# Feed-forward up in a two-layer encoder trunk: tokens instead of weights as the stationary operand, rows turned by VectorE and small DMAs

## The chip, the cores and the metric

The kernel runs on one core of one Trainium2 chip. The metric is the device time of one execution in microseconds (us); the time of the kernel before is the median of three runs. The profile is one more execution, recorded by the hardware profiler. Engines are named as in the profile: PE is TensorE, and PEld its loading of stationary operands; DVE is VectorE, ACT ScalarE, POOL GpSimd, and SP (SPq in the trace) is SyncE, which here issues nearly all DMAs.

## What is computed

Two layers, each with a mixer beside a cross-attention into 256 memory tokens, an output projection and a feed-forward part. Only the feed-forward part is touched: 256 tokens, width 2048, hidden width 8192, all float32.

```python
for layer in range(2):
    ...                                   # mixer, memory attention, output projection
    hn = rmsnorm(h, ffn_norm_g[layer])
    h = h + jnp.square(jax.nn.relu(hn @ ffn_w1[layer])) @ ffn_w2[layer]
return rmsnorm(h, final_norm_g)
```

## The kernel before

**Precision.** Each float32 operand is split into a high and a low float32r part, and each product is made of three matmuls: high by high, high by low, low by high. For weights, ACT writes the high part `w_hi` from the landed tile `raw` (`split`, L1072, the instruction is at L1077), and DVE subtracts to get `w_lo` (`split`, L1602, L1607).

**The weight stream.** SP loads weights as 128x512 tiles of 256 KB (`load`, L388; the DMA is at L397) into eight slots. Sixteen tiles (k-tiles, kt 0 to 15, eight slabs s of two) make a block. The load of k-tile kt waits until PE has used the k-tile eight before it (`tile_used`, L396). So SP runs at most eight k-tiles ahead of PE, and ACT and DVE follow, each strictly in program order: `head(B)` splits slabs 0 and 1 of block B, `tail(B)` slabs 2 to 7.

**The feed-forward part of a layer** (`ffn`; L957 on PE, L1486 on ACT, L2202 on DVE, L2397 on POOL; `stream_ffn`, L408, on SP) has two halves of 4096 hidden units. Each half has eight *up* blocks (512 hidden units each, 16 k-tiles) and eight *down* blocks (four column groups of two blocks). `R_FFN` and `B_FFN` number results and blocks.

- *Up* (`up_slab`, L552): the weight tile is the stationary operand, in four 128x128 pieces f. For each k-tile and piece there is a matmul of 512 columns (`w_hi` against high and low tokens side by side, L565) and one of 256 columns (`w_lo` against high tokens, L567). The result has hidden units on partitions and tokens along the row, as down wants it. Even blocks (j = 0) take all four result banks, odd blocks (j = 1) the four `aux` banks (`up_bank`, L325).
- *After an up block*: ACT copies the high-token half out of each of the four banks (`up_highs`, L1471, L1476), DVE adds the other half (`relu_result`, L2143, L2148) and applies relu and the tokens' 1/rms (L2158). That factor is needed along the row, so it is spread once per layer by two matmuls against a diagonal (`rstd_rows`, L571). POOL squares a 128x1024 tile (L2395), ACT writes its high part `hid_hi` (`hidden`, L1482) and DVE the low part `hid_lo` (`hidden`, L2172), during the next block.
- *Down* (`slab`, L534): the hidden tokens are stationary (128x128), and the weight tile streams as 512 columns; per k-tile six matmuls of 512 columns (two token halves m by three products, L546 to L548). Results go to two of four banks by turns, and DVE adds them into `h` (`add_result`, L2165).

The first up block of a layer (`first_up`) stands beside the last transposes of the normalised tokens (`refill`). `slab` is also what all other projections of the kernel use, with the tokens `xT_hi`, `xT_lo` as stationary operand.

Of the kernel before, what the change touches and what calls it, by code (L numbers as in the profile page):

```python
# [14 lines left out]
P = 128  # L15
D = 2048
SEQ = 256
# [96 lines left out]
A_RS0 = A_FN0 + 8  # L114
A_TN1 = A_RS0 + 1
# [5 lines left out]
A_RS = (A_RS0, A_FN1 + 8)  # L121
# [35 lines left out]
def encoder_trunk(nc, x, mem, x_columns, mem_columns, mem_gain_columns, consts, tok_norm_g, dn_w_in, dn_conv_w, dn_a_log, dn_dt_bias,  # L157
# [13 lines left out]
    with ctx:  # L171
# [127 lines left out]
        up_T = relu[:].rearrange("p j m (f t) -> p j (m f) t", f=2)  # L299
# [25 lines left out]
        def up_bank(R, j, f):  # L325

            return aux[f] if j else banks[(2 * (R % 2) + f) % 4]
# [59 lines left out]
        def _(sp):  # L387
# [20 lines left out]
            def stream_ffn(layer):  # L408
                with sp.Fori(0, 2) as half:
                    with sp.Fori(0, 8) as i:  # L410
                        for s in range(SLABS):
                            load(ffn_w1[layer], 0, half * (HID // 2) + i * NB, half * 16 + i + B_FFN[layer], s)
                    with sp.Fori(0, 4) as i:
                        for s in range(2 * SLABS):
                            B = half * 16 + i * 2 + (B_FFN[layer] + 8 + s // 8)
                            load(ffn_w2[layer], half * (HID // 2) + (s // 8) * D, i * NB, B, s % 8)

# [115 lines left out]
        def _(pe):  # L533
# [17 lines left out]

            def up_slab(B, s, R, parity, j, odd=None):  # L552

                for k in range(2):
                    kt = 2 * s + k
                    slot = kt % SLOTS
                    pe.wait_ge(tiles_split, B * 16 + (kt + 1))
                    for f in range(4):
                        if kt == 0 and j == 0:
                            pe.wait_ge(result_drained[f % 2], R + (f // 2 + 1))  # L560
                        elif kt == 0 and f == 0:
                            pe.wait_ge(sem("up_aux_free"), odd)
                        acc = up_bank(parity, j, f)
                        cols = slice(f * P, (f + 1) * P)
                        pe.matmul(acc[:], w_hi[:, slot, cols], xT[:, kt], start=kt == 0, stop=False,  # L565
                                  skip_group_check=True)
                        mm = pe.matmul(acc[:, 0:SEQ], w_lo[:, slot, cols], xT_hi[:, kt, :], start=False, stop=kt == KT - 1,  # L567
                                       skip_group_check=True)
                    mm.then_inc(tile_used, 1)

            def rstd_rows(layer):  # L571

                n = A_RS[layer]
                may_fill(pe, n)
                pe.wait_ge(sem("rstd_diagonal"), 2 * layer + 2)
                for m in range(2):
                    mm = pe.matmul(aux[n % 4][:, m * P:(m + 1) * P], ones, rstd_diag[:, m], start=True, stop=True)
                mm.then_inc(aux_filled[n % 4], 1)

            def first_up(layer):  # L580

                for s in range(SLABS):
                    drained(pe, ffn_fill[layer][s])
                    if s == SLABS - 1:
                        rstd_rows(layer)
                    up_slab(B_FFN[layer], s, R_FFN[layer], R_FFN[layer], 0)
                    yield
# [358 lines left out]
            def last_gates():  # L946

                for s in range(SLABS):
# [6 lines left out]
                         first_up(0)))  # L955

            def ffn(layer, next_steps, next_fill=None):  # L957


                for half in range(2):  # L960
                    def up(it, j):
                        b = it * 2 + j
                        for s in range(SLABS):
                            up_slab(half * 16 + b + B_FFN[layer], s, half * 12 + b + R_FFN[layer], R_FFN[layer], j,
                                    half * 16 + it * 4 + (32 * layer + 4) if j else None)
                    if half == 1:
                        up(0, 0)
                    if half == 0:
                        for n in range(4):
                            drained(pe, A_RS[layer] - n)  # L970
# [26 lines left out]
                    def down(i, c):  # L997

                        for s in range(16):
                            if (i, c) == (0, 0) and s % 2 == 0:  # L1000
                                pe.wait_ge(sem("hidden_split"), 16 * layer + 8 * half + s // 2 + 3)
# [61 lines left out]
            for n in (1, 2):  # L1063
                finish(out_block(n))
            beside(refill(ffn_fill[1], h, REFILL, R_OUT[1]),
                   chain(out_block(3), first_up(1)))
# [4 lines left out]
        def _(act):  # L1071
# [385 lines left out]
            def first_up(layer):  # L1457

                for t in range(SLABS):
                    split(B_FFN[layer] + (t + 2) // 8, (t + 2) % 8)  # L1460
                    if t == SLABS - 3:
                        norm_known(act, (N_FFN0, N_FFN1)[layer])
                        for m in range(2):
                            act.activation(rstd_diag[:, m], ident, ACT.Copy, scale=rstd[:, 0, m:m + 1]
                                           ).then_inc(sem("rstd_diagonal"), 1)
                    if t == SLABS - 1:
                        copy_aux(A_RS[layer], rstd_row, src=aux[A_RS[layer] % 4][:, 0:SEQ])
                        up_highs(layer, B_FFN[layer], 16 * layer, 0)
                    yield

            def up_highs(layer, B, n, j):  # L1471

                act.wait_ge(sem("hidden_split"), n + 1)
                result(act, B)
                for f in range(4):
                    act.activation(up_T[:, j, f, :], up_bank(R_FFN[layer], j, f)[:, 0:SEQ], ACT.Copy  # L1476
                                   ).then_inc(sem("up_high"), 1)

            beside(refill(ffn_fill[0], GN_FFN, REFILL_OUT, R_FFN[0]),
                   chain(out_part(8 * B_OUT[0] + 24, 8), first_up(0)))  # L1480

            def hidden(layer, half, it, j):  # L1482
                act.wait_ge(sem("squared"), half * 8 + it * 2 + (16 * layer + j + 1))
                act.activation(hid_hi[:, bass.ds(it * 8 + 4 * j, 4), :], up_T[:, j], ACT.Copy).then_inc(sem("hidden_hi"), 1)

            def ffn(layer, stages=None, next_steps=None):  # L1486
                for half in range(2):
                    def up(it, j, between):
                        tail(half * 16 + it * 2 + (B_FFN[layer] + j), between)
                        head(half * 16 + it * 2 + (B_FFN[layer] + j + 1))  # L1490
                        up_highs(layer, half * 16 + it * 2 + (B_FFN[layer] + j), half * 8 + it * 2 + (16 * layer + j), j)
                    if half == 1:
                        up(0, 0, None)
                    with act.Fori(0, 3) as it:
                        up(it, 1, lambda: hidden(layer, half, it, 0))
                        up(it + 1, 0, lambda: hidden(layer, half, it, 1))
                    up(3, 1, lambda: hidden(layer, half, 3, 0))
                    B = half * 16 + B_FFN[layer] + 8
                    tail(B, lambda: hidden(layer, half, 3, 1))
                    if half == 0:  # L1500
                        with act.Fori(0, 7) as i:
                            head(i + (B + 1))
                            tail(i + (B + 1))
                        head(B + 8)
                for i in range(3):
                    head(B + 1)
                    tail(B + 1)
                    head(B + 2)
# [67 lines left out]
            for n in (1, 2):  # L1576
                finish(block_steps(B_OUT[1] + n))
            beside(refill(ffn_fill[1], GN_FFN + 16, REFILL, R_FFN[1]),
                   chain(block_steps(B_OUT[1] + 3), first_up(1)))
# [14 lines left out]
        def _(dve):  # L1594
# [4 lines left out]
            dve.sem_inc(sem("up_aux_free"), 4)  # L1599
            dve.sem_inc(sem("hidden_split"), 2)  # L1600
# [542 lines left out]
            def relu_result(layer, n, R, j):  # L2143

                drained(dve, A_RS[layer])
                for f in range(4):
                    dve.wait_ge(sem("up_high"), 4 * n + (f + 1))
                    e = dve.tensor_tensor(up_T[:, j, f, :], up_T[:, j, f, :], up_bank(R_FFN[layer], j, f)[:, SEQ:], ALU.add)  # L2148
                    if j == 0:
                        free_result(e, f % 2)  # L2150
                    else:
                        e.then_inc(sem("up_aux_free"), 1)
                if j == 0:
                    for m in range(2):
                        dve.wait_ge(result_drained[m], R + 4)
                else:
                    dve.wait_ge(sem("up_aux_free"), 2 * n + 6)
                dve.scalar_tensor_tensor(out=up_T[:, j], in0=up_T[:, j], scalar=0.0, in1=over(rstd_row, 4),  # L2158
                                         op0=ALU.max, op1=ALU.mult).then_inc(sem("activated"), 1)

# [280 lines left out]
```

## Time and profile before

| | |
|---|---|
| median of 3 runs | 2309.48 us (2309.35 to 2315.8) |
| span of the profiled execution | 2308.9 us |
| PE busy | 2295.0 us, 99% |
| DVE, ACT, POOL busy | 1531.6 (66%), 1231.1 (53%), 114.3 us (5%) |
| HBM read | 419 MB, 182 GB/s over the span |
| granted TensorE clock | 0.999 of full speed (2.4 GHz) |

The span runs from the first to the last instruction of the profiled execution; its time and the median of the runs differ by 0.6 us. The page is read from the busy shares to the chain that ended last, then to the groups of instructions by line, and then, stage by stage, to the order of time.

### The profile page before, as it was taken

The numbers are of one execution on the slowest core, as the hardware profiler recorded it, in microseconds if no ns is written. First come the engines' busy times: TensorE is split into PE (matmuls) and PEld (weight loads), VectorE is DVE, ScalarE is ACT, GpSimd is POOL, SyncE is SP. The second block draws the span as 40 slices with busy tenths as digits, with TensorE's granted clock in tenths as the row PEclk, the third lists the DMA queues.
The fourth block names the chain that finished last, engine by engine and source line by source line (L and its number), as shares of the span: only waits on it lengthen the run. The fifth ranks groups of instructions, "written<-read, shape, count | busy, mean of one in ns | idle before, by whom it ended". The sixth has DMA issues, their size and how long they took to land.

```text
span 2308.9 us, 35429 instructions
## 1 busy us (share of the span) xinstructions
PE 2295.0 (99%) x11661; PEld 1945.0 (84%) x11661; DVE 1531.6 (66%) x2513; ACT 1231.1 (53%) x2277; POOL 114.3 (5%) x90
## 2 busy tenths in 40 slices
PE   9999999999999999999999999999999999999998
PEld 7888888888888888888888888888888888888887
DVE  6678788797767755567665555556767555677555
ACT  6566475564555544455544455545555444555544
POOL 0010100000001100001000000000101000001000
PEclk9999999999999999999999999999999999999999
DMA  9655364463566666666666675666666666666665
GB/s 327 185 156 163 112 170 140 134 185 111 162 189 188 190 193 193 192 186 185 185 193 194 188 214 158 168 190 196 188 189 190 193 194 192 189 190 189 194 193 176
DMA packets 232549, 422.82 MB, mean 183 GB/s; under 512 B 27884, under 2 KB 29805, under 8 KB 232301
## 3 DMA queue, kind: packets, MB, share of 16 engines
q1 hardware_dynamic: 231709, 420.15, 61.1%
q8 instruction: 77, 1.26, 0.2%
q10 hardware_dynamic: 720, 1.06, 0.1%
q14 instruction: 43, 0.35, 0.0%
HBM read 419.00 MB, written 2.10 MB: 182 GB/s over the span
## 4 chain that ended last, share of the span: by engine, by line
PE 94%; DVE 3%; ACT 1%; DMA 1%; issue 0%; SPq 0%; POOL 0%; POOLq 0%; ACTq 0%; DVEq 0%
PE pair L546 19%; PE pair L548 19%; PE pair L547 19%; PE pair L565 10%; PE aux L565 10%; PE aux L567 5%; PE pair L567 5%; PE aux L776 3%; PE aux L594 2%; DVE w_lo L1607 1%; DMA raw<-in_mem_w_kv 1%; DVE r L1934 1%; PE aux L823 0%; DVE attnT L1928 0%; DVE projections L1834 0%
## 5 line engine op out<-in xcount | busy, mean ns | idle before, releaser
L1607 DVE TENSOR_TENSOR w_lo<-raw,w_hi 128x512 fp32r<-128x512 f32 x1536 | 1077.6, 728 | 583.6 <-ACT w_hi L1077 580.9
L1077 ACT ACTIVATE w_hi<-raw 128x512 fp32r<-128x512 f32 x1536 | 939.9, 634 | 778.9 <-DMA raw<-in_ffn_w 619.9
L546 PE MATMUL pair<-w_hi,hid_hi 128*128 128x512 f32 x1012 | 394.3, 390 | 0.0
L548 PE MATMUL pair<-w_hi,hid_lo 128*128 128x512 f32 x1012 | 393.8, 389 | 0.0
L547 PE MATMUL pair<-w_lo,hid_hi 128*128 128x512 f32 x1012 | 393.8, 389 | 0.0
L546 PE MATMUL pair<-w_hi,xT 128*128 128x512 f32 x960 | 384.0, 400 | 3.3 <-DVE w_lo L1607 2.4
L548 PE MATMUL pair<-w_hi,xT 128*128 128x512 f32 x960 | 374.6, 390 | 0.0
L547 PE MATMUL pair<-w_lo,xT 128*128 128x512 f32 x960 | 374.1, 390 | 0.0
L565 PE MATMUL pair<-xT,w_hi 128*128 128x512 f32 x1024 | 359.6, 395 | 0.4 <-DVE h L2170 0.2
L565 PE MATMUL aux<-xT,w_hi 128*128 128x512 f32 x1024 | 357.4, 394 | 0.0
L567 PE MATMUL pair<-xT,w_lo 128*128 128x256 f32 x1024 | 286.3, 280 | 0.0
L567 PE MATMUL aux<-xT,w_lo 128*128 128x256 f32 x1024 | 286.2, 279 | 0.0
L565 PEld LDWEIGHTS pair<-xT,w_hi 128*128 128x128 f32 x1024 | 191.9, 187 | 46.4 <-DVE h L2170 2.2
L565 PEld LDWEIGHTS aux<-xT,w_hi 128*128 128x128 f32 x1024 | 191.8, 187 | 44.2
L548 PEld LDWEIGHTS pair<-w_hi,hid_lo 128*128 128x128 f32 x1012 | 189.9, 188 | 39.9
L546 PEld LDWEIGHTS pair<-w_hi,hid_hi 128*128 128x128 f32 x1012 | 190.0, 188 | 39.2
L547 PEld LDWEIGHTS pair<-w_lo,hid_hi 128*128 128x128 f32 x1012 | 190.0, 188 | 39.1
L546 PEld LDWEIGHTS pair<-w_hi,xT 128*128 128x128 f32 x960 | 180.5, 188 | 43.4 <-issue 5.1
L548 PEld LDWEIGHTS pair<-w_hi,xT 128*128 128x128 f32 x960 | 180.2, 188 | 38.7
L547 PEld LDWEIGHTS pair<-w_lo,xT 128*128 128x128 f32 x960 | 180.7, 188 | 34.4
L567 PEld LDWEIGHTS pair<-xT,w_lo 128*128 128x128 f32 x1024 | 193.2, 189 | 0.1
L567 PEld LDWEIGHTS aux<-xT,w_lo 128*128 128x128 f32 x1024 | 193.2, 189 | 0.0
(265 smaller groups left out, 1463.3 us busy)
## 6 DMA issues: line engine op xcount, KB each, us to landing
raw<-in_ffn_w SPq DMA_DIRECT2D x1024, 256.0 KB, 3.0
raw<-in_dn_w_in SPq DMA_DIRECT2D x208, 256.0 KB, 2.9
raw<-in_tok_w_out SPq DMA_DIRECT2D x128, 256.0 KB, 3.0
raw<-in_gm_w_in SPq DMA_DIRECT2D x112, 256.0 KB, 2.9
raw<-in_mem_w_kv SPq DMA_DIRECT2D x64, 256.0 KB, 3.2
r<-in_mem_columns SPq DMA_DIRECT2D x8, 256.0 KB, 5.6
h<-in_x_columns SPq DMA_DIRECT2D x8, 256.0 KB, 7.2
h<-in_mem_columns SPq DMA_DIRECT2D x8, 256.0 KB, 3.3
```

The lines of the kernel that those rows point to most:

```text
L546: pe.matmul(acc, act_hi[:, kt, tokens], w_hi[:, slot], start=start, stop=False)
L547: pe.matmul(acc, act_hi[:, kt, tokens], w_lo[:, slot], start=False, stop=False)
L548: mm = pe.matmul(acc, act_lo[:, kt, tokens], w_hi[:, slot], start=False, stop=last and k == 1)
L565: pe.matmul(acc[:], w_hi[:, slot, cols], xT[:, kt], start=kt == 0, stop=False, skip_group_check=True)
L567: mm = pe.matmul(acc[:, 0:SEQ], w_lo[:, slot, cols], xT_hi[:, kt, :], start=False, stop=kt == KT - 1, skip_group_check=True)
L594: t = pe.transpose(aux[n % 4][0:src.shape[1], col:col + w], src, cst[0:w, C_ID:C_ID + w])
L776: mm = pe.matmul(bank(n)[part, i * width:(i + 1) * width], lhs(i), rhs(i), start=True, stop=True)
L1077: act.activation(w_hi[:, slot], raw[:, slot], ACT.Copy).then_inc(hi_ready, 1)
L1607: dve.tensor_tensor(w_lo[:, slot], raw[:, slot], w_hi[:, slot].bitcast(F32), ALU.subtract).then_inc(tiles_split, 1)
L1934: e = dve.scalar_tensor_tensor(out=NT[:, d, m, hh, :], in0=view[:, k, 1, :], scalar=beta(m, d, hh), in1=NT[:, d, m, hh, :], op0=ALU.mult, ...
```

## The change

Up uses `slab`, the same six matmuls of 512 columns per k-tile as down, with the tokens stationary and the weights streaming. So an up result has tokens on partitions and hidden units along the row, in two banks by turns. What follows has to turn it:

- ACT evicts a result with relu and 1/rms in two 128x512 instructions (at s = 2 of the next block), into `up_rows`.
- POOL squares them in place, in two 128x512 halves.
- DVE transposes 32x32 squares of each half into `turned_rows` (at s = 5 and 6 of that next block).
- SP moves 32x32 squares between partition groups: 16 DMAs per block (`move_hidden`), each of 32 partitions with 1 KB, from `turned_rows` to `hidden_T`. They stand in SP's queue behind slabs 1 to 4 of the block two later, four at a time, and the first waits for both transposes. The last two blocks of a half are moved during the first two down blocks.
- ACT then writes `hid_hi` in two 128x512 halves (at s = 3 of the block two later, behind a wait for all 16 DMAs), and DVE `hid_lo` in two halves (at s = 4).

`rstd_rows`, `up_slab`, `first_up`, `up_highs` and `relu_result` are gone, and the `aux` slot of the spread factor too.

```diff
-        up_T = relu[:].rearrange("p j m (f t) -> p j (m f) t", f=2)
+        up_rows = relu[:].rearrange("p j m n -> p j (m n)").rearrange("p j (f m c) -> p j f m c", f=4, m=2)
+        turned_rows = xn_late[:, 0].rearrange("p (j a f m i) -> p j f m a i", j=2, a=4, f=4, m=2)
+        hidden_T = xn_late[:, 1].rearrange("p (j b f m i) -> p j m f b i", j=2, b=4, f=4, m=2)
...
@@ sync, stream_ffn @@
+                    with sp.Fori(0, 3) as it:
+                        for j in range(2):
+                            for s in up(it * 2 + (2 + j)):
+                                if 1 <= s < 5:
+                                    move_hidden(block_of(layer, half, j) + it * 2, half, j, s - 1)
+                    for s in down(0):
+                        if 1 <= s % 8 < 5:
+                            move_hidden(block_of(layer, half, 6 + s // 8), half, s // 8, s % 8 - 1)
...
+            def move_hidden(n, half, j, part):
+                if part == 0:
+                    sp.wait_ge(sem("rows_turned"), 2 * n + 2)
+                a = part
+                turned, moved = (xn_late[:, m, j * 2 * NB:(j + 1) * 2 * NB].rearrange("p (c y) -> p c y", c=4) for m in range(2))
+                for b in range(4):
+                    dst, src = moved[32 * a:32 * a + 32, b], turned[32 * b:32 * b + 32, a]
+                    sp.dma_start(dst, src).then_inc(sem(f"hidden_moved{half}{j}"), 16)
...
@@ tensor, ffn @@
-                            up_slab(half * 16 + b + B_FFN[layer], s, half * 12 + b + R_FFN[layer], R_FFN[layer], j,
-                                    half * 16 + it * 4 + (32 * layer + 4) if j else None)
+                            slab(b + (half * 16 + B_FFN[layer]), s, b + (half * 12 + R_FFN[layer]),
+                                 (R_FFN[layer] + j) % 2, 2 * s, xT_hi, xT_lo, s == 0, s == SLABS - 1)
...
@@ scalar @@
+            def up_tail(layer, half, B, last=None, before=None):
+                for s in range(2, SLABS):
+                    split(B, s)
+                    if s == 2 and last is not None:
+                        it, j = last
                         norm_known(act, (N_FFN0, N_FFN1)[layer])
+                        result(act, it * 2 + (half * 16 + B_FFN[layer] + j))
                         for m in range(2):
...
+                            rows = banks[2 * ((R_FFN[layer] + j) % 2) + m][:].rearrange("p (f c) -> p f c", f=4)
+                            free_result(act.activation(up_rows[:, j, :, m, :], rows, ACT.Relu, scale=rstd[:, 0, m:m + 1]), m)
+                    if s == 3 and before is not None:
+                        it, j = before
+                        act.wait_ge(sem(f"hidden_moved{half}{j}"), it * 256 + (1024 * layer + 256))
+                        tiles = hid_hi[:, bass.ds(it * 8 + 4 * j, 4), :].rearrange("p f (m b i) -> p m f b i", m=2, b=4)
+                        for m in range(2):
+                            act.activation(tiles[:, m], hidden_T[:, j, m], ACT.Copy).then_inc(sem("hidden_hi"), 1)
...
@@ vector @@
+            def up_tail(layer, half, B, last=None, before=None):
+                for s in range(2, SLABS):
+                    split(B, s)
+                    if s == 4 and before is not None:
+                        it, j = before
+                        high, low = (x[:, bass.ds(it * 8 + 4 * j, 4), :].rearrange("p f (m b i) -> p m f b i", m=2, b=4)
+                                     for x in (hid_hi, hid_lo))
+                        for m in range(2):
+                            dve.wait_ge(sem("hidden_hi"), it * 4 + (2 * block_of(layer, half, j) + m + 1))
+                            dve.tensor_tensor(low[:, m], hidden_T[:, j, m], high[:, m].bitcast(F32), ALU.subtract
+                                              ).then_inc(sem("hidden_split"), 1)
+                    if s in (5, 6) and last is not None:
+                        it, j = last
+                        m = s - 5
+                        dve.wait_ge(sem("squared"), it * 4 + (2 * block_of(layer, half, j) + m + 1))
+                        dve.transpose(turned_rows[:, j, :, m], up_rows[:, j, :, m, :].rearrange("p f (a i) -> p f a i", a=4)).then_inc(sem("rows_turned"), 1)
...
@@ gpsimd, square_hidden @@
+                            for m in range(2):
+                                pool.wait_ge(result_drained[m], half * 12 + it * 2 + (R_FFN[layer] + j + 3))
+                                t = up_rows[:, j, :, m, :]
+                                pool.tensor_tensor(t, t, t, ALU.mult).then_inc(sem("squared"), 1)
```

## Rows read from the trace of the kernel before

**Rows 1.** The page: engines' busy time, and the chain that ended last, by engine

```profile
PE 2295.0 (99%) x11661; PEld 1945.0 (84%) x11661; DVE 1531.6 (66%) x2513; ACT 1231.1 (53%) x2277; POOL 114.3 (5%) x90
...
PE 94%; DVE 3%; ACT 1%; DMA 1%; issue 0%; SPq 0%; POOL 0%; POOLq 0%; ACTq 0%; DVEq 0%
```

**Rows 2.** Order of time, PE, inside an up block: start, length (us), instruction

```profile
700.22 0.40 PE L565 MATMUL aux<-xT,w_hi 128*128 128x512 f32 x1
700.45 0.28 PE L567 MATMUL aux<-xT,w_lo 128*128 128x256 f32 x1
700.57 0.39 PE L565 MATMUL aux<-xT,w_hi 128*128 128x512 f32 x1
```

**Rows 3.** Single lines' instructions, and PE's order of time: starts of the stages

```profile
L565 PE MATMUL pair<-xT,w_hi x256: 392/395/500, 619.8 to 777.2; 128*128 128x512 f32 x128
...
L546 PE MATMUL pair<-w_hi,hid_hi x512: 389/389/481, 799.7 to 1331.7; 128*128 128x512 f32 x171
...
973.82 0.39 PE L565 MATMUL pair<-xT,w_hi 128*128 128x512 f32 x1
...
1155.30 0.40 PE L546 MATMUL pair<-w_hi,hid_hi 128*128 128x512 f32 x1
...
L565 PE MATMUL pair<-xT,w_hi x13: 389/398/496, 1594.8 to 1599.7; 128*128 128x512 f32 x13
...
L546 PE MATMUL pair<-w_hi,hid_hi x9: 387/389/391, 1774.4 to 1779.9; 128*128 128x512 f32 x9
...
L565 PE MATMUL pair<-xT,w_hi x64: 389/391/497, 1948.5 to 1971.0; 128*128 128x512 f32 x64
...
L546 PE MATMUL pair<-w_hi,hid_hi x244: 387/389/391, 2126.6 to 2291.9; 128*128 128x512 f32 x122
```

**Rows 4.** Order of time, PE, around the spread of 1/rms

```profile
641.18 0.60 PE L577 MATMUL aux<-rstd_both,cst 128*128 128x128 f32 x4
641.54 0.48 PE L565 MATMUL pair<-xT,w_hi 128*128 128x512 f32 x1
```

**Rows 5.** Who waited for whom: engine, line, releaser, total us, times, longest

```profile
PEld pair L565 <- DVE h L2170: 2.2, 6, 0.5
```

**Rows 6.** Line L397 in seven up blocks: SP's issues (ns min/median/max) and landing

```profile
L397 SPq DMA_DIRECT2D raw<-in_ffn_w x112: 332/333/343, 644.7 to 798.7; - x112
...
DMA to landing us min/median/max: 2.7/2.9/3.9
```

**Rows 7.** Order of time, SP, in the first 45 us: issues behind one another

```profile
2.59 0.91 SPq L397 DMA_DIRECT2D raw<-in_mem_w_kv  x2
...
7.18 0.74 SPq L435 DMA_DIRECT2D tok<-in_tok_norm_g  x1
7.96 0.42 SPq L435 DMA_DIRECT2D tok<-in_ffn_norm_g  x1
...
8.80 0.30 SPq L435 DMA_DIRECT2D tok<-in_gm_b_s  x1
9.14 0.37 SPq L436 DMA_DIRECT2D tok<-in_dn_conv_w  x1
...
43.32 0.43 SPq L459 DMA_DIRECT2D rows<-in_dn_a_log  x1
43.79 0.43 SPq L459 DMA_DIRECT2D rows<-in_dn_dt_bias  x1
```

**Rows 8.** Groups by line and shape: busy us, mean ns, idle before

```profile
L1607 DVE TENSOR_TENSOR w_lo<-raw,w_hi 128x512 fp32r<-128x512 f32 x1536 | 1077.6, 728 | 583.6 <-ACT w_hi L1077 580.9
L1077 ACT ACTIVATE w_hi<-raw 128x512 fp32r<-128x512 f32 x1536 | 939.9, 634 | 778.9 <-DMA raw<-in_ffn_w 619.9 <-DMA raw<-in_tok_w_out 55.6 <-DMA raw<-in_dn_w_in 42.1
...
L2395 POOL TENSOR_TENSOR relu<-relu 128x1024 f32<-128x1024 f32 x32 | 72.8, 2275 | 976.7 <-DVE relu L2158 976.7
...
L2158 DVE SCALAR_TENSOR_TENSOR relu<-relu,rstd_both 128x1024 f32<-128x1024 f32 x32 | 39.2, 1225 | 2.8 <-DVE relu L2148 0.9
```

**Rows 9.** Stretches: busy us by engine, granted clock, DMA share, GB/s (an up stage)

```profile
619.80:799.70 179.90, 179.90 (x1043) 157.31 (x1042) 127.86 (x182) 98.01 (x176) 17.42 (x9) 1.00 0.65 187
```

More of the change, by code:

```diff
@@ L113 @@
 A_FN0 = A_MIX0B + 2
-A_RS0 = A_FN0 + 8
-A_TN1 = A_RS0 + 1
+A_TN1 = A_FN0 + 8
 A_WS = A_TN1 + 8
@@ L323, in encoder_trunk, with block_of @@
         tok1_fill = [A_TN1 + p for p in range(8)]
-        def up_bank(R, j, f):
-            return aux[f] if j else banks[(2 * (R % 2) + f) % 4]
+        def block_of(layer, half, b):
+            return 16 * layer + 8 * half + b
         def filled(e, n, rounds=0):
@@ L550, in slab @@
                     mm.then_inc(tile_used, 1)
[L552 to L587, printed above, removed]
             def transposes(n, pieces, rounds=0):
@@ L1455, in _ @@
                                                 out_part(8 * B_OUT[0], 24)))
[L1457 to L1461, printed above, removed]
+            beside(refill(ffn_fill[0], GN_FFN, REFILL_OUT, R_FFN[0]),
+                   chain(out_part(8 * B_OUT[0] + 24, 8), block_steps(B_FFN[0])))
+            def up_tail(layer, half, B, last=None, before=None):
[3 more added lines that the diff above has]
+                        it, j = last
@@ L1469, in first_up @@
[L1469 to L1480, printed above, removed]
@@ L1486, in ffn, with up @@
             def ffn(layer, stages=None, next_steps=None):
                 for half in range(2):
[L1488 to L1491, printed above, removed]
+                    def up(b, last, before=None):
+                        up_tail(layer, half, b + (half * 16 + B_FFN[layer]), last, before)
+                        head(b + (half * 16 + B_FFN[layer] + 1))
@@ L1498, in ffn @@
                     B = half * 16 + B_FFN[layer] + 8
-                    tail(B, lambda: hidden(layer, half, 3, 1))
+                    up_tail(layer, half, B, (3, 1), (3, 0))
+                    head(B + 1)
+                    up_tail(layer, half, B + 1, None, (3, 1))
+                    head(B + 2)
                     if half == 0:
[L1501 to L1504, printed above, removed]
+                        with act.Fori(0, 6) as i:
+                            tail(i + (B + 2))
+                            head(i + (B + 3))
@@ L2141, in _ @@
             residual(dve, R_OUT[0] + 4)
[L2143 to L2159, printed above, removed]
             beside(refill(ffn_fill[0], GN_FFN, REFILL_OUT, 48, R_FFN[0]),
                    chain(out_part(PART_B, 8 * B_OUT[0] + 24, R_OUT[0] + 4),
-                         block_steps(B_FFN[0], lambda: relu_result(0, 0, R_FFN[0], 0))))
+                         block_steps(B_FFN[0])))
             def add_result(B, parity, i):
```

100 lines of the change are left out of this document (43 added, 57 removed).

## The prediction

> **What bounds the kernel now.** I read the page first: PE is busy for 99% of the span and carries 94% of the chain that ended last; no other engine is over 66% [rows 1]. So time can only be won by giving PE less to do, and is lost wherever PE has to wait. Next the order of time inside an up block [rows 2]: a 512-column matmul starts 0.23 us before its 256-column neighbour, and that one 0.12 us before the next. The lengths in that view overlap (0.40 and 0.28); only the distance of the starts is what a matmul costs. Last, the starts of the eight feed-forward stages [rows 3], which give the same distances as means over hundreds of matmuls.
>
> Layer 1, second up stage: 1948.5 to 2126.6, 178.1 us for 8 blocks x 16 k-tiles x 4 pieces = 512 pairs, 0.3479 us a pair. Layer 1, first down stage: 1774.4 to 1948.5, 174.1 us for 8 x 16 x 6 = 768 matmuls of 512 columns, 0.2267 us each. Both multiply the same number of columns (4 x 768 = 6 x 512 = 3072 per k-tile). At 2.4 GHz, the level granted there [rows 9], 512 columns are 213.3 ns and 768 are 320 ns. What stands over is 13.4 ns for one matmul and 27.9 ns for two: nearly the same for each instruction, whatever its width. Up pays it eight times per k-tile, down six times.
>
> **Part by part: PE.** Up becomes the six matmuls of down. Per k-tile 4 x 0.3479 = 1.392 us become 6 x 0.2267 = 1.360 us. By stages: 178.1 becomes 174.1, a gain of 4.0, in three of four up stages. In the second half of layer 0 both stages ran at a slower pace (973.8 to 1155.3 is 181.5; 1155.3 to 1332.4, three matmuls after its last high one, is 177.1): a gain of 4.4 there. Together 16.4 us. The matmuls that spread 1/rms go, 0.36 us in each layer [rows 4]: 0.7. An even up block needs all four result banks, so at the start of a second half it waits for DVE's `add_result`: 2.2 us in six waits of the weight loads [rows 5], mostly beside running matmuls. They go too, as `slab` needs only the two banks that are free; but since they are inside the 178.1 that I also applied to first halves, which have none, I take 0.5 off. **Sum on PE: 16.6 us**, if PE never waits. The span would go from 2308.9 to 2292.3, the median, which lies 0.6 higher, from 2309.5 to 2292.9.
>
> Here a rule speaks against the change. The Trainium skill (TensorE: Matmul & The Clock Gate, section "Back-to-back issue gap") gives the spacing of lone matmuls as N/2.4 + 2.5 ns, so 2.5 ns an instruction instead of some 14; worked out from that page, two matmuls fewer in each of 512 k-tiles would be worth an estimated 2.6 us. The trace disagrees: 226.7 ns measured where the formula gives 215.8.
>
> **Part by part: what feeds PE.** Everything else lies beside PE as long as the weight tiles keep coming. POOL: two squares of about 2.275 / 2 = 1.14 us [rows 8] instead of one; they start when ACT has evicted, some 2 us into the next block, and DVE wants them near 14 us: covered. If squares were late, DVE and then SP would be. ACT: two evictions and two halves of `hid_hi` at about 0.63 each, where four copies and one 128x1024 stood; no more work. DVE loses four additions and two passes of 1.23 per block, and gains two halves of `hid_lo` at 0.73 and two transposes. No row shows a transpose: the bounds are 0.73 (a 128x512 on DVE) and 1.23 (a 128x1024, if it runs at half pace) [rows 8]; a gain against 0.73 is excluded as it passes as many elements. I take 0.73, the row of equal shape.
>
> SP's queue is the new place. Before, it held 16 weight issues a block, 0.33 us each, in 21.8 us [rows 6]. Now 16 moves stand between them, four behind each of slabs 1 to 4, behind a wait for DVE's transposes. Queued behind that wait and the moves are the weight loads of k-tiles 4 to 15, for which ACT, DVE and PE wait. An issue behind another took 0.47 us (43.32 to 43.79), at the least 0.34 (8.80 to 9.14), at the most 0.78 (7.18 to 7.96); two weight loads took 0.91 and a gap of 0.04, so 0.475 each [rows 7]. I take 0.47 for a move, from issues with nothing slow ahead of them. 16 x 0.47 + 16 x 0.475 = 15.1 us of 21.8: it fits in sum. What matters is a **closed loop**, passed once a block: transposes done, moves, landing, `hid_hi`, `hid_lo`, next transposes. Each engine works in program order, so weight splits lie in it as well:
>
> - SP: 15 issues of 0.47 ahead of the last move, and six weight loads (k-tiles 4 to 9): 7.05 + 2.85 = 9.9.
> - Landing of the last move: 2.9, the median for weights (2.7 to 3.9) [rows 6]. No row shows a move inside SBUF; for less and for more I keep these ends.
> - ACT: two halves of `hid_hi` 1.27, splits of k-tiles 8 and 9 1.27.
> - DVE: split of k-tile 9 0.73, `hid_lo` 1.46, k-tiles 10 and 11 1.46, transpose 0.73, k-tiles 12 and 13 1.46, transpose 0.73.
>
> Sum 21.9 us, against a block of 16 x 1.360 = 21.8. So the loop is as long as the block itself. How long PE stays fed: k-tile 9 is loaded when k-tile 1 has been used, 2.7 us into the block, so the last move is issued near 4.7 and lands at 7.6; `hid_hi` ends at 8.9; DVE has split k-tile 9 at 11.0, `hid_lo` is done at 12.4 and k-tile 10 split at 13.15. PE wants it at 10 x 1.36 = 13.6: a slack of about 0.5 us. With e the loop's excess over 21.8, and seven passes from the first to the last of a half's eight blocks, a half loses 7e - 0.5. For e = 0.14 that is 0.5 us, 1.9 us over four halves. **Forecast: 2292.9 + 1.9 = 2295 us.**
>
> Its own bounds: a loop with moves of 0.34 is 2 us shorter and leaves 2293; a loop of 22.1 (e = 0.35) gives 7 x 0.35 - 0.5 = 2 per half, 2301. Without the slow pace of layer 0's second half (3.4 + 3.0 us in the two stages) the lower end is 2288.
>
> **The rivals.**
> *The loop sets the pace (slower).* It decides where a half loses its gain of 4.15: 7e - 0.5 = 4.15, e = 0.66, a loop of 22.4 us. Either upper end does this alone: transposes of 1.23 or a landing of 3.9 add 1.0, so e = 1.14, 7.5 us a half, 30 in all: 2323. Moves of 0.63, halfway to the upper end, add 2.4: e = 2.54, 17.3 a half, 2362; moves of 0.78 would give 2425. For it: the sum itself has no slack, and SP never had to issue so many. Against: 0.74 stands only where a slow DMA was ahead, and the quick rows (0.30, 0.37) are small transfers like the moves.
> *Part of the gain is eaten.* The same loop with e from 0.35 to 0.66: 2301 to 2309.
> *The DMA engines are the bound.* A block's moves add 16 x 32 = 512 pieces of 1 KB to 16 x 128 = 2048 of 2 KB. With a price per piece the DMA share goes from 0.65 [rows 9] to 0.81, with a price per byte to 0.73: neither is 1, so I expect only later landings. At 3.9 for weights, k-tile 8 (issued at 2) is there at 6 and waits for ACT until 8.9 anyway. If it bound nevertheless it would show as the loop's landing at 3.9: 2323. The Trainium skill (DMA: Bandwidth & Descriptors, section "Measured (HBM→SBUF, 128 partitions, SWDGE, issued from GpSimd)") says that transfers under 64 KB are ruled by their descriptors and wants 1 MiB; the moves are 32 KB. No run here shows such a transfer.
> *The change doesn't do what it says.* If a matmul's overhead went with its columns, 0.3479 would already be 1.5 x 0.2267 = 0.340 plus waiting that the new form keeps; then only the spread and the start waits are won: 2309.5 - 0.7 - 2 = 2307. Against it: two stretches of hundreds of matmuls agree on 13 to 14 ns each. The formula of the Trainium skill above would end in the same place.
>
> **How the numbers follow.** Forecast (2288 to 2301) 0.60; part eaten (2301 to 2309) 0.13; loop sets the pace, with the DMA engines as its cause among it, 0.24, most of it at 2312 to 2362; change without effect (2307) 0.03. About 0.3% (7 us) is what a measurement of this kernel can tell from no change. Faster than 2302.6: 0.60 and a little of the second case, 0.63. Within: the rest of the second, the fourth, and 0.04 of the third, 0.17. Slower than 2316.4: 0.20. The range goes from 2288 to 2316 and leaves out 0.20 above.
>
> **What would show it.** Right: up stages of 174 to 176 us, a first-to-first distance of 0.227 in them, ACT's wait for the moves at s = 3 ending before PE runs dry, PE's idle time still near nothing. Wrong on the price of a matmul: the distance is over 0.23 in up with no waits. Wrong on the loop: PE waits for `w_lo` of k-tiles 8 to 12 in blocks 2 to 7 of a half and in its first two down blocks; SP's move issues over 0.55, their landing over 3.5, or transposes over 1 us tell which term it was. What would make the prediction wrong most likely is SP's issue time for moves.

## The result, and the profile after

The changed kernel takes 2364.5 us (2361.7 to 2364.9), the kernel before 2310.8 in the same runs: a ratio of 1.0224, 95% interval 1.0209 to 1.0239. It is 2.2% slower. The forecast was 2295, and 2364 lies above the range's upper end of 2316; it is where the first rival put moves of 0.63 us (2362).

The page of the changed kernel: busy time, the chain that ended last (by engine, by line), three groups of instructions, and the moves' DMA issues (median us to landing).

```profile
span 2363.0 us, 32922 instructions
PE 2293.0 (97%) x10629; PEld 1899.5 (80%) x10629; DVE 1432.3 (61%) x2449; ACT 1233.8 (52%) x2239; POOL 106.9 (5%) x122
...
PE 73%; SPq 13%; DVE 4%; DMA 3%; ACT 3%; issue 3%; POOL 0%; ACTq 0%; POOLq 0%; DVEq 0%
PE pair L572 23%; PE pair L574 22%; PE pair L573 22%; SPq L442 9%; SPq L397 3%; PE aux L765 3%; DMA xn_late<-xn_late 3%; PE aux L583 2%; DVE w_lo L1584 2%; ACT hid_hi L1462 1%; ACT w_hi L1063 1%; DVE r L1911 1%; DMA raw<-in_mem_w_kv 1%; PE aux L812 0%; DVE attnT L1905 0%
...
L572 PE MATMUL pair<-w_hi,xT 128*128 128x512 f32 x1984 | 788.8, 398 | 46.8 <-DVE w_lo L1584 45.9
...
L1462 ACT ACTIVATE hid_hi<-xn_late 128x512 f32 (+1 forms) x64 | 36.8, 622 | 133.3 <-DMA xn_late<-xn_late 133.3
L2147 DVE STREAM_TRANSPOSE xn_late<-relu 128x512 f32<-128x512 f32 x64 | 45.0, 703 | 0.0
...
xn_late<-xn_late SPq DMA_DIRECT2D x512, 32.0 KB, 2.3
```

Against [rows 1], PE's share of the chain fell from 94% to 73%, and SP's queue, which had none, now holds 13%: 9% of it in line L442, the moves. The span outside PE's busy time was 13.9 us before and is 70.0 now. The next lines say who waits (total us, times, longest): PE for DVE's low weight parts, in 37 waits where the kernel before (first line) had 5, and ACT for the moves, once for each of the 32 up blocks. Of the 37, 32 lie in the feed-forward part, eight in each half.

```profile
PE pair L546 <- DVE w_lo L1607: 3.3, 5, 1.4
...
PE pair L572 <- DVE w_lo L1584: 59.8, 37, 3.3
...
ACT hid_hi L1462 <- DMA xn_late<-xn_late: 133.3, 32, 5.8
```

One block of the chain, in order of time (start, length, what), from where PE gets k-tile 8 after a wait to where it gets k-tile 8 of the next block. Matmuls, moves and loads between are left out.

```profile
701.75 0.70 DVE w_lo L1584
702.50 0.50 PE pair L572
...
708.03 0.24 PE pair L574
708.42 0.33 SPq L397
708.90 0.53 SPq L442
709.47 0.59 SPq L442
710.11 0.59 SPq L442
710.74 0.59 SPq L442
711.60 0.35 SPq L397
712.20 0.34 SPq L397
712.59 0.51 SPq L442
...
721.10 0.59 SPq L442
721.73 1.83 DMA xn_late<-xn_late
723.86 0.38 issue
724.24 0.61 ACT hid_hi L1462
724.85 0.53 ACT w_hi L1063
725.40 0.70 DVE w_lo L1584
726.14 0.50 PE pair L572
```

The pass takes 726.14 - 702.50 = 23.64 us, where PE alone needs 21.76 for a block. PE uses k-tiles 8 to 11 (24 matmuls, 5.8 us); that lets SP load k-tile 3 of the next block (708.42); then SP issues 15 moves and six loads in a row (708.90 to 721.73); the sixteenth move lands 1.83 us after its issue began; ACT, which stands at the moves, makes `hid_hi`, then splits k-tile 8; DVE splits it; PE goes on. Behind another move, a move's issue starts 0.62 to 0.64 us later (709.47, 710.11, 710.74), against 0.47 in [rows 7]; 0.625 is what the sums below take.

DVE's second transposes, those of the moves in this pass and those of the next pass, were done at 707.87 and 731.51:

```profile
707.17 0.70 DVE L2147 STREAM_TRANSPOSE xn_late<-relu 128x512 f32<-128x512 f32 x1
...
730.81 0.70 DVE L2147 STREAM_TRANSPOSE xn_late<-relu 128x512 f32<-128x512 f32 x1
```

### The profile page after: what moved, and what is told of

Its sections match the earlier page's. It is cut to its first block, busy times and chain, and to the rows that moved or that the text cites. A ratio compares the mean times of both kernels' runs of the same rounds, so it can differ in the third digit from the quotient of the medians.

```text
span 2363.0 us, 32922 instructions
## 1 busy us (share of the span) xinstructions
PE 2293.0 (97%) x10629; PEld 1899.5 (80%) x10629; DVE 1432.3 (61%) x2449; ACT 1233.8 (52%) x2239; POOL 106.9 (5%) x122
## 4 chain that ended last, share of the span: by engine, by line
PE 73%; SPq 13%; DVE 4%; DMA 3%; ACT 3%; issue 3%; POOL 0%; ACTq 0%; POOLq 0%; DVEq 0%
PE pair L572 23%; PE pair L574 22%; PE pair L573 22%; SPq L442 9%; SPq L397 3%; PE aux L765 3%; DMA xn_late<-xn_late 3%; PE aux L583 2%; DVE w_lo L1584 2%; ACT hid_hi L1462 1%; ACT w_hi L1063 1%; DVE r L1911 1%; DMA raw<-in_mem_w_kv 1%; PE aux L812 0%; DVE attnT L1905 0%
## 5 line engine op out<-in xcount | busy, mean ns | idle before, releaser
L1584 DVE TENSOR_TENSOR w_lo<-raw,w_hi 128x512 fp32r<-128x512 f32 x1536 | 1025.3, 693 | 803.5 <-ACT w_hi L1063 798.8
L572 PE MATMUL pair<-w_hi,xT 128*128 128x512 f32 x1984 | 788.8, 398 | 46.8 <-DVE w_lo L1584 45.9
L574 PE MATMUL pair<-w_hi,xT 128*128 128x512 f32 x1984 | 776.1, 391 | 0.0
L573 PE MATMUL pair<-w_lo,xT 128*128 128x512 f32 x1984 | 775.7, 391 | 0.0
L572 PEld LDWEIGHTS pair<-w_hi,xT 128*128 128x128 f32 x1984 | 374.5, 189 | 136.5 <-DVE w_lo L1584 57.2
L574 PEld LDWEIGHTS pair<-w_hi,xT 128*128 128x128 f32 x1984 | 374.1, 189 | 79.9
L573 PEld LDWEIGHTS pair<-w_lo,xT 128*128 128x128 f32 x1984 | 374.9, 189 | 74.3
L2373 POOL TENSOR_TENSOR relu<-relu 128x512 f32<-128x512 f32 x64 | 65.3, 1042 | 1033.0 <-ACT relu L1456 1033.0
L2147 DVE STREAM_TRANSPOSE xn_late<-relu 128x512 f32<-128x512 f32 x64 | 45.0, 703 | 0.0
L1811 DVE SCALAR_TENSOR_TENSOR r<-r,conv_w 128x256 f32<-128x256 f32 x96 | 40.0, 480 | 6.7 <-ACT r L1251 6.7
L2141 DVE TENSOR_TENSOR hid_lo<-xn_late,hid_hi 128x512 f32 (+1 forms) x64 | 41.1, 684 | 0.0
L1456 ACT ACTIVATE relu<-pair,rstd 128x512 f32<-128x512 f32 x64 | 40.0, 676 | 0.0
L1105 ACT ACTIVATE xT<-aux,gains 128x256 fp32r<-128x256 f32 x48 | 19.8, 472 | 33.7 <-PE aux L583 33.7
```

Of the source, the lines that this page charges most:

```text
L572: pe.matmul(acc, act_hi[:, kt, tokens], w_hi[:, slot], start=start, stop=False)
L573: pe.matmul(acc, act_hi[:, kt, tokens], w_lo[:, slot], start=False, stop=False)
L574: mm = pe.matmul(acc, act_lo[:, kt, tokens], w_hi[:, slot], start=False, stop=last and k == 1)
L1584: dve.tensor_tensor(w_lo[:, slot], raw[:, slot], w_hi[:, slot].bitcast(F32), ALU.subtract).then_inc(tiles_split, 1)
L2147: dve.transpose(turned_rows[:, j, :, m], up_rows[:, j, :, m, :].rearrange("p f (a i) -> p f a i", a=4)).then_inc(sem("rows_turned"), 1)
L2373: pool.tensor_tensor(t, t, t, ALU.mult).then_inc(sem("squared"), 1)
```

## The experiments

Two theories stood first. **A**: the time is SP's, 16 issues in a row at 0.6 us, with weight loads queued among them and ACT's splits queued behind the wait for them. **B**: it is the DMA engines', the moved bytes. All times below are beside runs of the kernel before on the same chip.

**Leaving the moves out** (`e1_no_moves`). The first down blocks and DVE's `hid_lo` are changed in the same way.

```diff
-                                    move_hidden(block_of(layer, half, j) + it * 2, half, j, s - 1)
+                                    pass
...
-                        act.wait_ge(sem(f"hidden_moved{half}{j}"), it * 256 + (1024 * layer + 256))
+                        act.wait_ge(sem("rows_turned"), it * 4 + (2 * block_of(layer, half, j) + 2))
...
-                            act.activation(tiles[:, m], hidden_T[:, j, m], ACT.Copy).then_inc(sem("hidden_hi"), 1)
+                            act.activation(tiles[:, m], turned_rows[:, j, :, m], ACT.Copy).then_inc(sem("hidden_hi"), 1)
```

> The 16 moves per block are left out (the high and low hidden parts are made from the turned rows, so squares stand in wrong partition groups); all else stays. Theory A, SP's queue: in the changed kernel 16 issues of about 0.6 us and the landing of the last hold ACT ahead of k-tile 8, and nothing else is lost; without them up runs at down's pace: 2292 to 2297. Theory B, the moves' bytes load the DMA engines: the same here. Theory C, the price of a matmul was wrong, or transposes and squares in program order hold DVE up: 2305 or more, with PE waits left in up blocks.

Measured: 2289.4 us against 2312.7, ratio 0.9901 (0.9884 to 0.9918), 2.6 us below the expected band. Busy time, and a down stage and the up stage behind it, each from its first matmul to the next stage's (length, then busy us of PE, PEld, DVE, ACT and POOL, granted clock, DMA share, GB/s):

```profile
PE 2273.2 (99%) x10629; PEld 1895.3 (83%) x10629; DVE 1473.5 (64%) x2449; ACT 1238.0 (54%) x2239; POOL 106.9 (5%) x122
...
793.75:967.83 174.08, 174.08 (x770) 144.19 (x769) 95.82 (x140) 83.76 (x134) 2.04 (x2) 1.00 0.63 194
967.83:1141.90 174.07, 174.07 (x769) 144.19 (x768) 109.77 (x156) 93.86 (x154) 14.29 (x14) 1.00 0.68 193
```

Up and down take the same 174.1 us, PE is busy throughout. So the evictions, squares, transposes and half-width copies cost PE no time, the gain on PE is there in full, and all 75 us between 2289 and 2364 hang on the moves. In the two profiles the span differs by 76.3 us (2363.0 against 2286.7): 56.5 is more time without a matmul (70.0 against 13.5), 19.8 is longer matmuls (2293.0 against 2273.2 busy), of which more below.

**How many, and how large** (`e3_eight_moves`, `e10_twelve_moves`, `e4_half_bytes`, `e14_twenty_moves`). Fewer moves leave out the last two, or the last, of each four (`for b in range(2)`, `range(3)`); the half-size run moves 128 elements a row instead of 256; the last one adds a fifth:

```diff
                     sp.dma_start(dst, src).then_inc(sem(f"hidden_moved{half}{j}"), 16)
+                sp.dma_start(spare[32 * a:32 * a + 32, :], turned[0:32, a, 0:HALF]).then_inc(sem(f"hidden_moved{half}{j}"), 16)
```

> Eight of the 16 moves per block are left out (half of the hidden values are stale), each of the rest as large as before. Theory A: eight issues of 0.62 us fewer, 5.0 us, more than the 1.9 us by which a block is too long: no PE waits are left, 2293 to 2297. Theory B: half the moved bytes are left, so about half of the 70 us: near 2330.

> Four of the 16 moves per block are left out (a quarter of the hidden values are stale). By theory A, with a point from which it decides: the loop shrinks by 4 x 0.625 = 2.5 us, more than its excess of 1.9, so the whole loss goes and not a quarter: 2289 to 2296. If each move cost the same 70 / 16 = 4.4 us: 2347.

> All 16 moves per block stay, but each carries 512 bytes per partition instead of 1 KB (half of the hidden values are stale). Theory A: the number of issues sets the time, so 2358 to 2366. Theory B, bytes: near 2330, as with eight moves.

> The changed kernel with four more moves per block, one behind each of slabs 1 to 4 (64 elements a row, into a spare tile that nobody reads). Theory A: past the point from which the loop decides, each issue costs its whole time: 4 x 0.625 = 2.5 us a block, some 28 to 32 passes, so 70 to 80 us more: 2430 to 2445. If SP's queue still had room, or if the bytes counted (6% more): within 10 us of 2364.

| moves per block | bytes per block | us (before in the same runs) |
|---|---|---|
| 0 | 0 | 2289.4 (2312.7) |
| 8 | 256 KB | 2289.3 (2312.7) |
| 12 | 384 KB | 2291.8 (2309.7) |
| 16, as changed | 512 KB | 2364.5 (2310.8) |
| 16, half rows | 256 KB | 2359.2 (2312.7) |
| 20 | 544 KB | 2484.9 (2313.1) |

Eight moves and sixteen half moves carry the same bytes, and differ by 70 us: B falls. (Eight came out 4 us below the expected band, twelve and the half moves inside theirs.) Twelve moves are nearly free and sixteen cost 75 us: there is a point from which the loop decides, and it lies between. Past it, four more moves cost 120 us where A had 70 to 80. The profile of that run shows why. The span outside PE's busy time grew by 74.8 us (144.8 against 70.0), as A had it; the other 46.4 are PE's busy time (2339.4 against 2293.0): after the longer waits its matmuls themselves ran slower (last section). A block there takes 27.7 us, 4.0 more and not 2.5 (PE's 24 matmuls of k-tiles 8 to 11 take 7.4 us of it, 735.87 to 743.23, instead of 5.8), as SP's order of time shows (the first moves of two blocks), and the last line is the stretch of one block (length, then busy us of PE, PEld, DVE, ACT and POOL, granted clock, DMA share, GB/s):

```profile
716.18 2.45 SPq L443 DMA_DIRECT2D xn_late<-xn_late  x4
...
743.87 2.41 SPq L443 DMA_DIRECT2D xn_late<-xn_late  x4
...
724.00:748.00 24.00, 19.99 (x81) 16.13 (x80) 11.71 (x19) 10.28 (x18) 2.04 (x2) 0.93 0.57 171
```

**Using the moved rows later** (`e2_late_wait`). Every move stays where it was; ACT comes to them at s = 6 and DVE at s = 7, behind the transposes (s = 5 and 6 in the last block of a half).

```diff
-                    if s == 3 and before is not None:
+                    if s == (5 if early else 6) and before is not None:
...
-                    if s == 4 and before is not None:
...
+                    if s == (6 if early else 7) and before is not None:
```

> All moves stay, where they were in SP's queue; only their use is put later in the block: the high hidden part at s = 6 (5 in the second down block) instead of 3, the low part at s = 7 (6) instead of 4, behind the transposes. Theory A1, the loss is ACT's wait for the moves, which stands ahead of the weight splits of k-tiles 8 and 9: that wait falls to nearly nothing, PE wants k-tile 10 at 13.6 us and has it at about 13.0: 2293 to 2302. Theory A2, the loss is SP's issues alone, which bring the weight tiles late whoever waits: at least half of the 70 us between 2293 and 2364 stays, 2330 or more. Theory B, DMA engines: the landing of weights and moves stays what it was, 2330 or more.

Measured: 2307.8 us against 2312.7, ratio 0.9977 (0.9968 to 0.9987), above the expected band. Of the 75 us, 57 go, with no DMA taken away: what cost most was the place of the use, ACT's weight splits behind a wait for the moves. (DVE's order was changed with it; the run `e13_early_turn` below changes DVE's order alone, and gains nothing.) The rest is seen in who PE waited for:

```profile
PE pair L572 <- DVE w_lo L1584: 7.7, 17, 1.4
PE pair L572 <- DVE hid_lo L2146: 7.3, 4, 2.1
```

The four waits for `hid_lo` are the last block of each half, used too late by my own edit. The 17 for `w_lo` are the other part (four of them, 3.0 us, stand in the run without moves too): SP takes 3.69 us for four moves and two loads (708.90 to 712.59 in the chain above), PE uses the two k-tiles in 2.72, so loads fall behind whoever waits.

**Spreading them** (`e11_spread`). The late use, with three moves behind each of slabs 1 to 5 and one behind slab 6, and the last block of a half used at s = 4 and 5.

```diff
+                for k in range(each * (s - 1), min(each * s, 16)):
+                    a, b = k // 4, k % 4
```

> All moves and the late use, with two edits: three moves behind each of slabs 1 to 5 and one behind slab 6, instead of four behind each of 1 to 4 (a group then takes SP 3.1 us per slab instead of 3.7; PE uses a slab in 2.7), and the last block of a half used at s = 4 and 5 instead of 5 and 6. Theory A: the weight tiles fall behind by 5 x 0.4 = 2 us instead of 4 x 0.95 = 3.8, and the 17 waits for low weight parts of the late-use run (17 us) and the four for the last hidden part (9 us) go: 2289 to 2297. If the rest of the loss in that run had another cause than SP's pace: 2303 or more.

Measured: 2289.4 us against 2309.7, ratio 0.9914 (0.9895 to 0.9933): the whole loss is gone with nothing left out.

**Other queues** (`e7_two_queues`, `e5_pool_queue`). In the first, SP keeps moves b = 0 and 1, and ACT issues b = 2 and 3, four behind each of its splits of slabs 0 and 1; their use stays where the change put it. In the second, GpSimd issues all 16, behind its squares.

```diff
+                for s, parts in ((0, (0, 1)), (1, (2, 3))):
+                    split(B, s)
+                    if last is not None:
+                        move_rest(j, half, parts)
```

> The same 16 moves of the same bytes, and their use where the change put it; but eight of them are issued from ACT's queue, behind its splits of slabs 0 and 1. ACT has 9 us a block free and pays 8 x 0.6 = 5 of them. Theory A, issues in a row on SP: SP's part of the loop shrinks by 5.0 us as with eight moves, 2289 to 2297, with nothing left out. Theory B, the engines behind the queues: no better than 2355. Rival: ACT, in program order, gets too late with its splits: PE waits for the low weight parts of k-tiles 2 to 6, 2310 or more.

> All 16 moves go from SP's queue to GpSimd's, which has 20 us a block free; their use stays where the change put it. Theory A: SP is as free as before; if an issue there takes up to 0.6 us, the last lands as late as now but no weight tile does, and only ACT's wait is left: 2300 to 2350. If GpSimd's issues take 1 us or more, 16 of them are the loop: 2400 or more. Theory B, engines: 2364 as now.

Measured: 2288.8 us against 2309.7, ratio 0.9910 (0.9891 to 0.9929) with two queues (at the lower end of the band); 2295.0, ratio 0.9937 (0.9913 to 0.9962), with GpSimd's. GpSimd's issues were quicker than I had allowed for, as its order of time shows (start, length, engine, line):

```profile
699.22 7.87 POOL L2369 DMA_DIRECT2D xn_late<-xn_late  x16 [9.26 <-DVE xn_late L2137]
```

That is 0.49 us each, so the last one lands early, and the time is below the expected band. Same moves, same bytes; what differs is whose time the issues take, and that the moves no longer stand between weight loads. Landing was no quicker: medians of 2.7 and 3.0 us from SP and ACT, and 2.9 from GpSimd, against 2.3 in the changed kernel. This settles A against B. The Trainium skill (DMA: Bandwidth & Descriptors, section "Issuing engines are not separate DMA queues") says that issuing from several engines only saves the sequencers' time, usually small beside the DMA; the first half agrees with both runs, and the second does not hold here, where an issue took 0.59 us of the 2.3 until a move landed, and the issues together 16 x 0.625 = 10 us of a 21.8 us block.

The GpSimd run is 6 us behind the other (5.6 between the profiles), and this lies behind the work: PE's last matmul ends at 2279.5 us in it and at 2279.1 in the two-queue run, but the program's last instructions come behind GpSimd's closing DRAIN, which takes 11.1 us (2281.2 to 2292.4) where it takes 0.67 in the two-queue run:

```profile
L169 POOLq DRAIN  x1: 11131/11131/11131, 2281.2 to 2281.2; - x1
...
L169 POOLq DRAIN  x1: 665/665/665, 2280.9 to 2280.9; - x1
```

**Which loop** (`e13_early_turn`). Only the transposes are moved forward.

```diff
-                    if s in (5, 6) and last is not None:
+                    if s in (3, 4) and last is not None:
                         it, j = last
-                        m = s - 5
+                        m = s - 3
```

> The changed kernel with only DVE's two transposes moved forward, to s = 3 and 4 instead of 5 and 6; nothing is left out. The loop of the prediction ran through the transposes (transposes, moves, landing, high part, low part, four splits, transposes): if it is the one that sets the pace, it gets 4 splits, 2.7 us, shorter, and the time falls to 2300 or less. Theory A as the trace of the changed kernel reads: SP stands at k-tile 3 until PE has used the k-tile eight earlier, and the transposes are done by then: no change, 2358 to 2368.

Measured: 2370.5 us against 2313.1, ratio 1.0249 (1.0219 to 1.0279), 2 us above the expected band. A block takes 23.9 us, from the first move of one block in SP's queue to that of the next:

```profile
708.65 2.43 SPq L442 DMA_DIRECT2D xn_late<-xn_late  x4
...
732.59 2.41 SPq L442 DMA_DIRECT2D xn_late<-xn_late  x4
```

There is no gain (the interval overlaps that of the changed kernel, so a loss is not shown either): the transposes, and with them the loop of the prediction, do not set the pace.

**What a move's issue costs, and why** (`e12_prices`). The two-queue kernel, and behind its last store five groups of four DMAs, issued by SP with nothing else running.

```diff
+            price("price_groups", [(raw[32:64, i, 0:256], xn_late[64:96, 0, i * 256:(i + 1) * 256]) for i in four])
+            price("price_same", [(raw[32:64, i, 256:512], xn_late[32:64, 0, i * 256:(i + 1) * 256]) for i in four])
+            price("price_all", [(raw[:, i, 0:256], xn_late[:, 0, i * 256:(i + 1) * 256]) for i in four])
+            price("price_hbm32", [(raw[0:32, 4 + i, 0:256], ffn_w1[0][32 * i:32 * i + 32, 0:256]) for i in four])
+            price("price_hbm128", [(raw[:, 4 + i], ffn_w1[0][P * i:P * i + P, 0:NB]) for i in four])
```

> The two-queue kernel, and behind its last store five groups of four DMAs, each group issued in a row by SP and waited for, with nothing else running: 32 rows of 1 KB from SBUF to SBUF between partition groups (a move), the same inside one group, 128 rows of 1 KB from SBUF to SBUF, 32 rows of 1 KB from HBM, 128 rows of 2 KB from HBM. It adds some 20 us at the end, which is not what is asked. Why did a move's issue take 0.59 us and not the 0.43 of the rows before? If it is the place (both ends in SBUF), the first three groups take 0.5 to 0.6 each and the last two 0.33 to 0.43. If it is the small number of rows, groups 1, 2 and 4 are at 0.5 to 0.6. If it is the other partition group, only the first. If it is the busy queue in the middle of the kernel, all are below 0.45.

The run's time holds the five groups and is not compared. Issues in stretches of its end (ns min/median/max, first and last start), one line for each group in that order:

```profile
L558 SPq DMA_DIRECT2D raw<-xn_late x1: 592/592/592, 2288.7 to 2288.7; - x1
...
L558 SPq DMA_DIRECT2D raw<-xn_late x3: 507/590/592, 2291.2 to 2292.4; - x3
...
L558 SPq DMA_DIRECT2D raw<-xn_late x3: 601/601/602, 2295.5 to 2296.8; - x3
...
L558 SPq DMA_DIRECT2D raw<-in_ffn_w x3: 421/421/423, 2299.3 to 2300.3; - x3
...
L558 SPq DMA_DIRECT2D raw<-in_ffn_w x2: 432/432/432, 2302.9 to 2303.3; - x2
```

Behind another one, an issue from SBUF to SBUF takes 0.59 to 0.60 us, with 32 rows or 128, inside a partition group or between two; from HBM 0.42 to 0.43, with 32 rows or 128. It is the place, not the rows, the partition group, or the busy kernel around it. And it is both places together, not the source alone: the kernel's own stores go from SBUF to HBM, and SP's four of them took 0.33 to 0.42 us in this run:

```profile
L554 SPq DMA_DIRECT2D out<-xn_late x4: 332/382/423, 2278.8 to 2283.3; - x4
```

## Why the prediction was wrong, step by step

- **The price of a matmul: right.** The step said 178.1 us for an up stage becomes 174.1; without the moves it is 174.1. The whole gain on PE was larger than the 16.6 of the sum: 22.2 us between the two profiles (2308.9 against 2286.7). Some 3.0 of the difference is layer 0's second half: up went there from 181.5 us [rows 3] to 174.1, and not to 177.1 as the sum had it. I had read the 177.1 of its down stage as a slow pace as well, and this reading was wrong: 24 small matmuls of line L594, which belong to the next layer, stand in that stage, and it takes 177.0 us in the run without moves too (first line: the kernel before; second: this stage without moves).

```profile
L594 PE MATMUL aux<-cst,h x24: 270/272/273, 1313.1 to 1329.5; 128*128 128x128 f32 x24
...
1141.90:1318.88 176.98, 176.98 (x793) 146.54 (x792) 99.80 (x152) 87.75 (x148) 2.04 (x2) 1.00 0.61 191
```

What made up slow there in the profile before stays open; the granted clock was 1.00. The remaining 2.6 us were not traced. The rule that the prediction weighed against this step gave 2.6 us for all stages, and one stage alone gained 4.0: it falls, and with it the rival that rested on the same doubt.
- **POOL, ACT, DVE: right.** The transpose, for which there was no row, took 0.703 us where I took 0.73 and allowed 1.23.
- **The price of a move's issue: the step that failed.** I took 0.47 us from issues that read HBM and kept 0.34 to 0.78 as ends; it was about 0.625. For 15 moves and six loads the sum had 9.9 us of SP, and the chain has 12.8 (708.90 to 721.73): 15 x 0.155 = 2.3 of the difference are the moves, the rest the gaps beside the loads. The sum had no slack to take it. With moves of 0.47 the pass of 23.64 us would be about 21.3 (an estimate), shorter than a block, and nothing would have been lost, as with twelve moves. All issues of [rows 7] read HBM; a move has both ends in SBUF, which no row showed.
- **The landing** was 2.3 us in the median, and 1.83 for the last move of the pass above, where I took 2.9; it hid 1.1 of the 2.9 us that SP's part was over.
- **The loop: right that one decides, wrong which.** I closed it through the transposes and counted the other way only as PE's slack of 0.5 us. In the trace the transposes are done (707.87) before SP comes to the moves (708.90); what holds SP is k-tile 3, which may be loaded only when PE has used k-tile 11. So the loop goes through PE's own matmuls, and moving the transposes forward changed nothing. The prediction's loop, with what its parts measured, is 22.6 us (from 708.90 to the second transpose's end at 731.51), a microsecond less than the pass: on it the price of the moves would have cost some 22 us by the prediction's formula (e = 0.85, 2315), and that the pass goes through PE, and that PE's matmuls slow down after waits, make the rest.
- **The signs.** Two of those named came out: PE's waits for `w_lo`, eight in each half, and issues over 0.55. The landing and the transposes stayed below theirs.
- **The rival's formula.** With moves of 0.63 it gave 2362 and 2364 was measured, but much of that is luck. Its excess of 2.54 us a block belongs to a loop that does not decide, and whose other parts were shorter than taken. The measured excess is 1.88, there are eight waits in a half where the formula has seven passes (56.5 us without a matmul in all), and the 20 us of longer matmuls were in no case of mine.
- **The chances.** 0.24 for the loop was too little, since the sum itself came out at 21.9 against 21.8. A forecast without slack should have taken both sides as about even.

## What to carry to other kernels

Count DMA issues as work of the engine that issues them: so many by the price of an issue of the same kind (with both ends in SBUF, or with one in HBM), against the time between two loads of the same queue, not only against the block. Where an engine works in order, put a wait for a long chain behind the work that others need, and close every loop through the slot that frees the next load. With that the same change is worth 0.9%: eight moves on another queue (2288.8 us) or the same moves spread and used later (2289.4) beat both kernels, where the change as made lost 2.2%.

## What the runs showed of the hardware that I had not expected

**Both ends in SBUF.** Behind another one, a DMA's issue on SP took 0.59 us from SBUF to SBUF (32 KB) and 0.60 (128 KB), 0.42 from HBM (32 KB) and 0.43 (256 KB); stores from SBUF to HBM took 0.33 to 0.42. From SBUF to SBUF it took 0.61 on ACT's queue (median of 256) and 0.50 on GpSimd. Halving the bytes of a move took its landing from 2.3 to 2.2 us and left its issue at 0.59: at these sizes the price of a move is almost all fixed.

**GpSimd's queue at the end.** With the moves on GpSimd, its closing DRAIN took 11.1 us instead of 0.67, which is most of the 6 us by which that run is behind.

**The clock after a wait.** In the changed kernel PE's matmuls are longer in some places. PE's order of time after a wait of 2.46 us (in brackets):

```profile
677.48 0.79 PE L572 MATMUL pair<-w_hi,xT 128*128 128x512 f32 x1 [2.46 <-DVE w_lo L1584]
...
678.49 0.63 PE L574 MATMUL pair<-w_hi,xT 128*128 128x512 f32 x1
678.92 0.63 PE L572 MATMUL pair<-w_hi,xT 128*128 128x512 f32 x1
...
681.33 0.39 PE L573 MATMUL pair<-w_lo,xT 128*128 128x512 f32 x1
...
```

The stretch around it (length, then busy us of PE, PEld, DVE, ACT and POOL, granted clock, DMA share, GB/s):

```profile
676.00:688.00 12.00, 10.53 (x40) 8.59 (x41) 9.28 (x15) 7.06 (x13) 0.00 (x0) 0.86 0.66 205
```

Starts lie 0.43 us apart (678.49, 678.92), which is 512 columns at 1.2 GHz, and 0.23 again from 680.9 on; the granted clock of the stretch is 0.86. After a wait of 1.52 us, at 702.50, they stayed at 0.23. The length of a wait alone does not tell which it will be: after one of 1.86 us, which ended at 1041.95, the clock fell, after one of 2.96, which ended at 1163.33, it did not (length, PE's busy us, granted clock, DMA share, GB/s):

```profile
1036.00:1048.00 12.00, 10.14 (x39) 0.86 0.66 208
1160.00:1172.00 12.00, 9.04 (x40) 1.00 0.70 226
```

So a wait of PE can cost more than its length. Here 56.5 us were without a matmul, and matmuls were 19.8 us longer. The granted clock is 0.86 in six stretches of 12 us cut around such places (from 676, 1036, 1792, 1840, 2044 and 2164), which makes an estimated 6 x 0.14 x 12 = 10 us; most of the rest is the 0.50 us that the first matmul after a wait takes in the chain where others take 0.23 (32 x 0.27 = 8.6). In the run with 20 moves, where waits reach 5 us, the clock fell to 0.93 over whole stretches and PE's busy time rose to 2339 us.
